# Filling products on TensorE taken out of the seams behind the result norms of a ten-block transformer kernel

## The reference

```python
for layer in range(2):                      # first model
    h = rms_norm(x, norm_mix_g[layer])
    x = x + (even_mixer(h, ...) if layer == 0 else gla_mixer(h, ...))
    h = rms_norm(x, norm_ffn_g[layer])
    x = x + conv_ffn(h, ...)                # (silu(conv(h @ w_gate)) * (h @ w_up)) @ w_down
for l in range(2):                          # second model
    h = swiglu(rms_norm_2(x, ffn1_norm_pre[l]), ...)
    x = x + 0.5 * rms_norm_2(h, ffn1_norm_post[l])
    h = hybrid_mixer(rms_norm_2(x, mix_norm_pre[l]), ...)
    x = x + rms_norm_2(h, mix_norm_post[l])
    h = swiglu(rms_norm_2(x, ffn2_norm_pre[l]), ...)
    x = x + 0.5 * rms_norm_2(h, ffn2_norm_post[l])
```

## Time and profile before

| | us |
|---|---|
| three runs | 3255.26, 3256.09, 3259.43 |
| median | 3256.09 |
| profiled execution, its own time | 3255.3 |
| its span, first to last instruction | 3253.5 |
| PE busy (15940 products) | 3199.3 (98%) |
| PEld busy | 2635.0 (81%) |
| DVE busy | 1181.5 (36%) |
| ACT busy | 1177.6 (36%) |
| POOL busy | 1466.1 (45%) |
| mean granted TensorE clock | 0.996 |

### The profile page before, as it was taken

One profiled execution on the slowest core, in us unless ns is written; L12 is line 12 of the kernel. 1 busy time (PEld: TensorE's weight loads), 2 busy tenths in 40 slices (PEclk: granted clock), 3 DMA queues, 4 the chain that ended last, 5 costly groups with the idle time before them and its releaser, 6 DMA issues.

```text
span 3253.5 us, 39586 instructions
## 1 busy us (share of the span) xinstructions
PE 3199.3 (98%) x15940; PEld 2635.0 (81%) x15940; DVE 1181.5 (36%) x1727; ACT 1177.6 (36%) x1388; POOL 1466.1 (45%) x1112
## 2 busy tenths in 40 slices
PE   8999999999999999999999999999999999999998
PEld 7878888888888888888786888888888877788887
DVE  6534431344443212210757522114221384752212
ACT  4544432433433222322427433224322343742322
POOL 4335454433555445445560354444444382054443
PEclk9999999999999999999999999999999999999999
DMA  4213223211222222222330132222222241022222
GB/s 149 77 53 108 99 93 115 95 65 65 91 103 90 104 104 95 99 104 104 114 113 22 52 117 90 103 104 91 90 103 104 78 165 69 14 91 91 102 102 92
DMA packets 46234, 302.56 MB, mean 93 GB/s; under 512 B 5392, under 2 KB 7440, under 8 KB 10784
## 3 DMA queue, kind: packets, MB, share of 16 engines
q1 hardware_dynamic: 41040, 292.79, 25.1%
q10 hardware_dynamic: 5072, 7.96, 0.8%
HBM read 296.54 MB, written 2.10 MB: 92 GB/s over the span
## 4 chain that ended last, share of the span: by engine, by line
PE 91%; DVE 6%; ACT 2%; issue 1%; DMA 0%; SPq 0%; DVEq 0%; ACTq 0%
PE main L424 73%; PE main L441 3%; PE main L567 2%; PE main L1907 1%; PE main L526 1%; PE main L527 1%; PE main L531 1%; PE misc L526 1%; PE misc L531 1%; PE misc L527 1%; PE misc L484 1%; ACT b_p L2061 1%; PE misc L499 1%; DVE b_p L2283 1%; DVE b_flat L2146 1%
## 5 line engine op out<-in xcount | busy, mean ns | idle before, releaser
L2379 POOL TENSOR_TENSOR w_lo<-stage,w_hi 128x512 fp32r<-128x512 f32 x1104 | 1460.0, 1356 | 1752.8 <-ACT w_hi L637 1752.8
L424 PE MATMUL main<-h_hi,w_lo 128*128 128x512 f32 x2456 | 964.8, 393 | 7.2 <-DVE val L2093 5.5
L424 PE MATMUL main<-h_lo,w_hi 128*128 128x512 f32 x2456 | 959.2, 391 | 0.0
L424 PE MATMUL main<-h_hi,w_hi 128*128 128x512 f32 x2456 | 959.2, 391 | 0.0
L637 ACT ACTIVATE w_hi<-stage 128x2048 fp32r<-128x2048 f32 x276 | 525.3, 1911 | 422.8 <-DMA stage<-in_w 422.0
L424 PEld LDWEIGHTS main<-h_hi,w_lo 128*128 128x128 f32 x2456 | 463.3, 189 | 109.5 <-DVE val L2093 6.0
L424 PEld LDWEIGHTS main<-h_hi,w_hi 128*128 128x128 f32 x2456 | 463.1, 189 | 97.3
L424 PEld LDWEIGHTS main<-h_lo,w_hi 128*128 128x128 f32 x2456 | 463.3, 189 | 95.2 <-issue 0.5
L424 PE MATMUL main<-hid_hi,w_lo 128*128 128x512 f32 x1168 | 454.5, 389 | 0.0
L424 PE MATMUL main<-hid_hi,w_hi 128*128 128x512 f32 x1168 | 454.4, 389 | 0.0
L424 PE MATMUL main<-hid_lo,w_hi 128*128 128x512 f32 x1168 | 454.4, 389 | 0.0
(11 more groups left out here) (337 smaller groups left out, 3198.0 us busy)
## 6 DMA issues: line engine op xcount, KB each, us to landing
stage<-in_w SPq DMA_DIRECT2D x276, 1024.0 KB, 4.8
x<-in_xT SPq DMA_DIRECT2D x4, 512.0 KB, 7.6
out_x<-x ACTq DMA_DIRECT2D x4, 512.0 KB, 2.7
stage<-in_w SPq DMA_DIRECT2D x4, 256.0 KB, 7.8
b_r<-sq ACTq DMA_DIRECT2D x4, 256.0 KB, 6.7
b_r<-sq ACTq DMA_DIRECT2D x4, 255.5 KB, 7.9
ev_ws<-in_ev_ws ACTq DMA_DIRECT2D x1, 512.0 KB, 4.4
b_pos<-in_pos ACTq DMA_DIRECT2D x2, 256.0 KB, 2.8
```

The costliest lines, as they stand in the source:

```text
L424: last = pe.matmul(acc[:, m, :], w[a], r[b], start=start and k == 0 and j == 0, stop=stop and k == nk - 1 and j == 2)
L2379: last = e.tensor_tensor(c.w_lo[:, s, k:k + 2, :].rearrange("p k n -> p (k n)"), c.stage[:, s, k * CW:(k + 2) * CW], c.w_hi[:, s, k:k + 2, ...
```

## The change

The calls of `keep_busy` in `last_sums` go. The call at the program's start and the function itself stay.

```diff
@@ -586,9 +586,7 @@
 
     pe.wait_ge(c.p_sqb, n(c.p_sqb, 4))
     token_sums(pe, c.m[0], c.ones, c.sq[:, 1, :], False, True).then_inc(c.ssq_ready, 1)
-    keep_busy(pe, c, 5)
     spread(pe, n, c)
-    keep_busy(pe, c, 9)
```

## The result

| | before | after |
|---|---|---|
| median of the runs | 3257.86 us (7) | 3267.82 us (7) |
| profiled execution | 3255.3 us | 3267.8 us |
| its span | 3253.5 us | 3266.0 us |
| mean granted TensorE clock | 0.996 | 0.988 |

The ratio is 1.0032, with a 95% interval of 1.0022 to 1.0042: 7 to 14 us slower. The forecast was +7.35 us, and 10 us is what the medians show. The direction and the mechanism are as forecast; the loss of a seam was put too low. The profiled execution of before lies 2.6 us under its median and that of after at its median, so the two spans differ by 12.5 us and not by 10.

The account below looks back on a forecast made before the run. The prediction took TensorE (PE), 91% of the chain that ended last, to bound the kernel. A 1.9 us gain and 9.25 us clock loss summed to +7.35 on 3256.09: 3263.4 us, range 3256 to 3268.

Parts of the forecast that it names:

- The gain of the five: Without five fills ahead of each seam's spread, the spread comes 0.32 us earlier: 6 x 0.32 = 1.9 us gained.
- The nine cost nothing where they stand: Nine fills behind each spread end before h is ready, PE idling 0.34 us already; taking them out gains nothing.
- A fall in each of the five seams: Without cover, the granted clock falls to 0.50 in each seam with a projection behind it: 5 x 1.85 = 9.25 us.
- PE-bound first pair, all of a loss passes on: First pair of chunks after a seam: PE busy 22.60 of 22.6 us, so it ends late by all PE lost.
- 0.47 us for each microsecond of wide products at 0.50: Wide products start 0.425 us apart instead of 0.225 at the low level, losing 0.47 us per microsecond of PE-bound work.
- How much of a stay meets wide products: Share of a 3.4 us low-clock stay over wide products behind a seam: between nothing and two stays, 3.2 us; 1.85 taken.
- one stay and a little: Loss assumed for each of five seams, 1.85 us, where a whole stay over wide products costs 1.6 us.
- my case: Clock falls in five seams, costing 1.3 to 2.5 us each: 3260.7 to 3266.7 us, chance 0.62.
- In all six falls with work behind them one stay was enough: Argument from the trace of before against two low-clock stays in each seam, which would add 14.1 us.
- my upper bound of 3.2: Most a seam could lose, in us: two stays in a row, without the spread's possible 1.06 us at half rate.
- The third rival: Two low-clock stays in each of five seams: 5 x 3.2 - 1.9 = +14.1 us, 3270.2 us; chance 0.15.
- The rule on idle gaps: Seam waits, 2.35 us and shorter, are under the skill's limit, so the clock would hold gap by gap; prediction rejected this.

Follow-up runs that it names:

- Three and nine: Kernel before with three instead of five filling products ahead of the spread and nine still behind it: 3255.22 us against 3258.11, ratio 0.9991.
- The fourteen fills: Kernel before with three filling products ahead of the spread instead of five and fourteen behind it instead of nine: 3259.66 us against 3257.71, ratio 1.0009.
- the sixth experiment: Kernel before with three fills ahead and nine behind in the seams, plus fills in the linear attention and gated attention waits: 3251.43 us against 3257.71, ratio 0.9981.

## Why the prediction was right and where it was wrong

*The gain of the five.* Right. The load moved from 2.00 to 1.69 us in all six seams, and where the clock held until the spread (seams two, four and six) VectorE got it at 2.88 instead of 3.21. Three and nine give it alone.

*The nine cost nothing where they stand.* Right: 5.20 to the first wide product with nine, 5.19 with none.

*A fall in each of the five seams.* Right, in both profiles of the change. What decides whether a seam with only the five or only the nine has a fall stays open.

*PE-bound first pair, all of a loss passes on.* Right. The fourteen fills showed it with the clock at 1.00: 0.53 us in, 0.55 us out.

*0.47 us for each microsecond of wide products at 0.50.* Right, within 0.03 us in each seam.

*How much of a stay meets wide products: this is the step that failed.* I took 1.85 us a seam, "one stay and a little", and bounded my case at 2.5. The net losses average 2.31 us, with the gain of 0.32 added 2.63, which is outside my case. Two things were in it.

First, a fall in the wait was followed by a second stay in every seam and a third in one, so that 2.9 to 5.9 us of wide products, 4.7 on average, ran at 0.50: 2.2 us a seam. "In all six falls with work behind them one stay was enough" was true of before, but at those falls products of 128 columns or more were under way, with no long wait behind them, or came at most 0.6 us later; here the wide products came 1.1 to 4.4 us later, and a wait lay between. Other falls agree. In the profile after, two outside the seams, at 677.60 and 2650.51, came 0.7 us ahead of wide products and lasted 6.8 us. With the nine fills behind the spread all three falls of the seams lasted 3.4 us. No run varied this delay by itself.

Second, I left the spread out of the sum, holding that a fall before the spread is early for both. In three of the five seams the fall came at or in the spread, which then took up to 1 us longer, and VectorE had it 0.6 to 0.9 us after the 2.88 of a full clock, 0.44 on average over the five. The first seam had both at once, a slow spread and 5.9 us of slow wide products: 3.34 + 0.32 = 3.7 us, over my upper bound of 3.2. 2.2 + 0.44 = 2.6.

The third rival, two stays in each seam, had the count right, but it priced both stays wholly over wide products, which gave +14.1 us; the measured +10 lies between it and my case. The time forecast was off by 4.4 us (3263.4 against 3267.8): 2.6 from the change, and 1.8 because the median of seven runs of before, 3257.86, lies above that of the three that I started from.

*The rule on idle gaps.* The Trainium skill ("TensorE: Matmul & The Clock Gate", section "Why this matters for your kernels") sets a limit to the idle gap between bursts of matmuls, and the longest gap in these seams, 2.35 us, is under it. Read gap by gap, the clock should have held. The rows contradict that reading for this kernel: five falls in each of two profiles with that gap, and with the one-column fills five falls with no gap over 0.7 us. With only the five ahead the gap was the same 2.35 us and three of five seams held. And with more cover (the sixth experiment) PE idled 3.04 us before 1605.2, with the clock at 1.00 on either side.

## What to carry to other kernels

Filling products are worth their place where an engine-bound stretch follows a wait that the clock doesn't survive; here fourteen in each of six waits were worth 10 us of 3258. Their width matters: those of 128 columns held the clock, and those of one column, with the same weight loads, did not. Ahead of a dependent step put only as many as are done before its operand comes (three here, where five cost 0.3 us each time), behind it as many as the wait holds; what lasts past the wait is paid in full where the work behind it has no slack. When costing the loss of such cover, count the whole low stretch from the fall to the return, what of it lies over bound work, and the small steps in the wait that run slow as well, and don't take the length of the stays from places where the work resumed at once.

## What the runs showed of the hardware

The low level slows weight loads too: eight loads of the spread, each followed by a product of 128 columns, took 1.77 us instead of 0.97, and eighteen of the fills 3.96 instead of 2.09, even with products of one column. Apart from the one at the program's end, the low stretches were 3.4, 6.8 or 10.2 us long in all nine profiles. And with PE recorded busy for all of 6.20 us, mostly by one-column products, the granted clock was 0.50: the busy row of PE doesn't tell whether the clock will hold.
